# Filler matmuls between the two norms ahead of a feed-forward are left out

## The reference

```python
def rms_norm(x, g):
    y = xf * lax.rsqrt(jnp.mean(xf * xf, axis=-1, keepdims=True) + RMS_EPS)
    return (y * g.astype(jnp.float32)).astype(x.dtype)

def modulated_norm(x, g, shift, scale):
    return rms_norm(x, g) * (1 + scale) + shift

def half_step_ffn(x, g_pre, g_post, shift, scale, gate, w_gate, w_up, w_down):
    h = modulated_norm(x, g_pre, shift, scale)
    y = (jax.nn.silu(h @ w_gate) * (h @ w_up)) @ w_down
    return x + FFN_RES * gate * rms_norm(y, g_post)
```

## Time and profile before

| | us |
|---|---|
| median of 3 timed runs | 1490.08 |
| lowest, highest | 1487.72, 1493.79 |
| span of the profiled execution (no other time of it is given) | 1499.0 |
| TensorE busy in it | 1434.4 (96%) |
| VectorE busy | 979.7 (65%) |
| ScalarE busy | 621.3 (41%) |
| GpSimd busy | 121.2 (8%) |
| mean granted TensorE clock | 0.979 of full speed |

### The profile page before, as it was taken

One profiled execution on the slowest core, in us unless ns is written; L12 is line 12 of the kernel. 1 busy time (PEld: TensorE's weight loads), 2 busy tenths in 40 slices (PEclk: granted clock), 3 DMA queues, 4 the chain that ended last, 5 costly groups with the idle time before them and its releaser, 6 DMA issues.

```text
span 1499.0 us, 27870 instructions
## 1 busy us (share of the span) xinstructions
PE 1434.4 (96%) x10570; PEld 1310.5 (87%) x10570; DVE 979.7 (65%) x1425; ACT 621.3 (41%) x951; POOL 121.2 (8%) x200
## 2 busy tenths in 40 slices
PE   7899999999999999999999999999999989999997
PEld 2699999999899976589999989999876878899996
DVE  2677677777676824458787878755685785755554
ACT  2433232323465623345444455444435432544442
POOL 2000001111004002101111101100000020000000
PEclk9999999999999988999999999999999998999999
DMA  8455547777557532038888857856432432266651
GB/s 331 155 182 186 179 154 225 240 250 238 176 162 186 159 92 74 11 115 260 288 303 289 291 181 243 281 180 185 149 113 62 150 127 84 77 192 182 182 176 48
DMA packets 74482, 268.26 MB, mean 179 GB/s; under 512 B 9018, under 2 KB 9573, under 8 KB 73840
## 3 DMA queue, kind: packets, MB, share of 16 engines
q1 hardware_dynamic: 52128, 187.03, 38.4%
q0 software_dynamic: 22288, 80.30, 16.8%
HBM read 266.25 MB, written 1.05 MB: 178 GB/s over the span
## 4 chain that ended last, share of the span: by engine, by line
PE 68%; DVE 13%; issue 7%; ACT 6%; DMA 6%; DVEq 0%; ACTq 0%; SPq 0%; POOL 0%; POOLq 0%
PE gu L1372 13%; PE gu L1374 13%; PE gu L1373 13%; PE acc L1372 5%; PE acc L1374 5%; PE acc L1373 5%; DMA raw<-in_wstream_dram 5%; DVE wlo L801 4%; ACT whi L434 4%; PE mean_p L1414 2%; DVE part L818 1%; PE acc L1640 1%; DVE rstd L866 1%; PE gu L1481 1%; PE acc L1757 1%
## 5 line engine op out<-in xcount | busy, mean ns | idle before, releaser
L801 DVE TENSOR_TENSOR wlo<-raw,whi 128x1024 fp32r<-128x1024 f32 x350 | 432.9, 1242 | 284.4 <-ACT whi L434 282.9
L1372 PE MATMUL gu<-h_lat_hi,whi 128*128 128x256 f32 x1760 | 506.8, 288 | 11.6 <-DVE h_lat_lo L910 4.1
L434 ACT ACTIVATE whi<-raw 128x1024 fp32r<-128x1024 f32 x350 | 366.8, 1053 | 333.6 <-PE gu L1374 144.2
L1373 PE MATMUL gu<-h_lat_lo,whi 128*128 128x256 f32 x1760 | 500.1, 284 | 0.0
L1374 PE MATMUL gu<-h_lat_hi,wlo 128*128 128x256 f32 x1760 | 500.0, 284 | 0.0
L1372 PEld LDWEIGHTS gu<-h_lat_hi,whi 128*128 128x128 f32 x1760 | 339.8, 193 | 29.5 <-issue 17.7
L1373 PEld LDWEIGHTS gu<-h_lat_lo,whi 128*128 128x128 f32 x1760 | 340.0, 193 | 2.3 <-issue 1.7
L1374 PEld LDWEIGHTS gu<-h_lat_hi,wlo 128*128 128x128 f32 x1760 | 339.9, 193 | 0.0
L1372 PE MATMUL acc<-act_hi,whi 128*128 128x256 f32 x880 | 250.8, 285 | 3.3 <-DVE z L1140 2.6
L1373 PE MATMUL acc<-act_lo,whi 128*128 128x256 f32 x880 | 249.6, 284 | 0.0
L1374 PE MATMUL acc<-act_hi,wlo 128*128 128x256 f32 x880 | 249.5, 284 | 0.0
(11 more groups left out here) (193 smaller groups left out, 1466.2 us busy)
## 6 DMA issues: line engine op xcount, KB each, us to landing
raw<-in_wstream_dram SPq DMA_DIRECT2D x350, 512.0 KB, 4.0
wm<-in_wmod_dram POOLq DMA_DIRECT2D x136, 512.0 KB, 5.1
area<-in_wmod_dram POOLq DMA_DIRECT2D x8, 512.0 KB, 8.0
area<-in_rpb_dram POOLq DMA_DIRECT2D x32, 64.0 KB, 3.1
x_lat<-in_x_in_dram SPq DMA_DIRECT2D x1, 1024.0 KB, 8.6
area<-in_ctx_in_dram SPq DMA_DIRECT2D x1, 1024.0 KB, 12.0
area<-in_dft_in_dram POOLq DMA_DIRECT2D x1, 1024.0 KB, 8.3
area<-in_window_in_dram POOLq DMA_DIRECT2D x1, 1024.0 KB, 11.4
```

The source lines that it names most:

```text
L434: nc.scalar.activation(whi[:, phase % RING, :], raw[:, phase % RAW, :], ACT.Copy).then_inc(hi_done, 1)
L801: nc.vector.tensor_tensor(wlo[:, u.base % RING, :], raw[:, u.base % RAW, :], whi[:, u.base % RING, :].bitcast(F32), ALU.subtract).then_inc ...
L1372: nc.tensor.matmul(out_, w_hi, x_hi, start=start, stop=False, skip_group_check=True)
L1373: nc.tensor.matmul(out_, w_hi, x_lo, start=False, stop=False, skip_group_check=True)
```

## The change

The function `keep_warm`, its six calls and the constant with their number are taken out. Nothing else differs.

```diff
-            def keep_warm(n):
-
-                for _ in range(n):
-                    nc.tensor.matmul(gu[:, 1, 0:P], mean_mat[:, :], mean_mat[:, :], start=True, stop=True)
-
...
             out_projection(U_ABO, 0, (4, 5, 6, 7, 0, 1, 2, 3))
             mean_of(6)
-            keep_warm(WARM[0])
             mean_of(7)
-            keep_warm(WARM[1])
             ffn(1, 4, 4 * (6 - LATE + 1))
             mean_of(8)
             batch_columns(1)
             pe.wait_ge(act_mul, 3 * FT)
-            keep_warm(WARM[0])
             mean_of(9)
-            keep_warm(WARM[1])
...
             out_projection(U_HYO, 8, range(KT))
             mean_of(12)
-            keep_warm(WARM[0])
             mean_of(13)
-            keep_warm(WARM[1])
             ffn(3, 7, 4 * (12 - LATE + 1))
...
-WARM = [18, 18]
```

## The result

| | us |
|---|---|
| before, median of 11 runs | 1491.21 (1487.72 to 1496.37) |
| without the fillers, median of 11 runs | 1500.81 (1493.07 to 1511.07) |
| ratio, with 95% interval | 1.0052 (1.0032 to 1.0072) |

The kernel became slower by 0.52%, 7.8 us (4.8 to 10.7 us); the medians lie 9.6 us apart. The forecast was 1499.7 us, in a range of 1491 to 1504 us.

What follows compares the result with a forecast made beforehand. The prediction took TensorE, busy 96% of the span, as the bound, with the fillers off the path. Clock lags of 1.1 + 2.1 us at three places add 9.6 us to 1490.1 us: 1499.7 us, range 1491 to 1504 us.

Steps and rivals of the forecast that it cites:

- What bounds the kernel, and the direct price: Norm chain on VectorE and ScalarE paces the three places; the fillers' 25 us of TensorE lie in waits, worth zero.
- A fall in all six holes: Without fillers, TensorE idles 4.5 to 5.3 us twice at each of three places; the granted clock falls every time.
- How long the low clock lasts: From restart to rise under dense matmuls: 4.8 us, the mean of four natural cases; bounds 2.6 and 5.5 us.
- Term 1: Second norm's 16 sums at each place, run at the low clock: a lag of 1.1 us a place.
- Term 2: First matmuls of each feed-forward after a place, 0.2135 instead of 0.12 us each: a lag of 2.1 us.
- What gives it back: Later slack in the feed-forwards, weight stream included, was claimed to recover nothing of the lag.
- Sum: 1.1 + 2.1 = 3.2 us for each place, 9.6 us for three; low 3.5 us, high 11.7 us.
- The estimate of 14.4 us: Skill's rule, half the throttled time: (4.8 + 4.8) / 2 = 4.8 us a place, 14.4 us in all.
- No cost: Rival: holes don't lower the clock where it matters, or the weight stream absorbs the lag; 1490 us, chance 0.09.
- The low clock stays longer: Rival: 9.6 us of low clock at each feed-forward and sums that never warm up; 19 us, 1509 us, chance 0.09.
- Faster: Rival: a filler batch delays the real matmul behind it, likeliest at the second place; removal gives 1484 us, chance 0.03.

Runs made afterwards that it cites:

- e4_long: Kernel before with 28 fillers instead of 18 in every batch; 1497.79 us, ratio 1.0026 to the kernel before.
- e2_first_only: Kernel before with only the second filler batch of each pair left out, the first batches kept; 1501.20 us, ratio 1.0042.
- e6_late: Kernel before with 34 fillers instead of 18 in the first place's second batch, all others kept; 1495.11 us, ratio 1.0013.
- e7_place1: Kernel before with both filler batches left out at the first of the three places alone; 1497.20 us, ratio 1.0017.
- e5_half: Kernel before with 9 fillers instead of 18 in every batch; 1500.59 us, ratio 1.0055.

## Why the prediction came out right, and where it didn't

**What bounds the kernel, and the direct price.** The prediction had the fillers off the path and worth nothing themselves. Right: every other distance in the places is unchanged to 0.01 us, and e4_long shows a cost only once a batch sticks out.

**A fall in all six holes.** Right, in both profiles of the change; once, at the second place, it came 0.4 us behind the hole. The holes measured 5.17, 5.02, 4.42, 5.02, 5.17 and 5.02 us.

**How long the low clock lasts.** This step was mis-sized. I took 4.8 us from four natural rises and held it for both terms. At the start of the feed-forwards it was 4.2, 3.4 and 3.2 us in the profile of the change, and 4.1, 3.2 and 3.2 us in the second one, 3.6 us on average; from the start of the sums to the rise it was 3.2 to 5.3 us, 4.1 us on average. Three of my four rises stood behind a start that was not dense from its first record (a fall after the restart, thin matmuls, one more hole). I had counted from the restart, and at 395 us that takes in 1.4 us at the full clock: the low stretch runs from 396.4 to 399.8 us, 3.4 us and not 4.8 us.

**Term 1, the sums.** Predicted 1.1 us a place, measured 0.73 us on average over six, from 0.29 to 1.29 us. The mechanism is as told: the groups grow together and the pace of the squares hides a part, and 3.3 us of low clock over the sums at the third place leave only 0.31 us of lag.

**Term 2, the start of the feed-forward.** Predicted 2.1 us, measured 1.56 us on average, from 1.40 to 1.84 us. The rate was right: 4.2 us of low clock times (1 - 0.12 / 0.2135) gives 1.84 us, which is what the first silu shows. Only the length was off.

**What gives it back.** Predicted nothing. Right for the last feed-forward, to 0.01 us. In the feed-forward after the first place nothing was given back either; profiles with a late start are 2.3 us longer there on top of the lag. I had seen that its weight stream is nearly as slow as TensorE, and asked only whether it could absorb the lag. In `ffn(2)` the averages late and on time are alike but for the lag.

**Sum.** Predicted 3 x (1.1 + 2.1) = 9.6 us. Measured by the lags 3 x (0.73 + 1.56) = 6.9 us; the timed ratios say 7.8 us (4.8 to 10.7) and 9.1 us (4.8 to 13.5). So both terms were too large, by a third and by a half, because of the length of the low clock, and that the median came within 1.1 us of the forecast is luck. The 2.3 us seen in `ffn(1)` would bring the lags to 9.2 us; the intervals hold 6.9 and 9.2 us alike, so the timed runs don't say whether it belongs in the sum. The estimate of 14.4 us by half of the throttled time (the Trainium skill, "TensorE: Matmul & The Clock Gate", section "Terms") is above both intervals. With the lengths measured behind the two restarts, 4.1 and 3.6 us, the same rule gives an estimate of some 11.5 us, above the first interval and inside the second.

**Rivals.** "No cost" is excluded by the intervals of both runs of the change. "The low clock stays longer" didn't occur: the longest low stretch at a feed-forward's start was 5.2 us (e2_first_only, first place). "Faster" needed a batch that sticks out; at 18 fillers none does.

**What stays open.** Whether a late start costs 2.3 us in `ffn(1)`, and how, was not shown: the groups part there, `ffn(2)` does not follow, and the timed runs of e6_late and e7_place1 lie nearer to no such term. What stands out is that GpSimd's first load of modulation weights in that stretch is issued by VectorE's progress and not by TensorE's: it came 0.7 us before the first silu when the start was on time and earlier by the lag when it was late (1.7 to 3.0 us before it). The waits of TensorE that its view lists there come to 0 to 0.4 us on time and 0 to 1.1 us late, less than the 2.3 us. That the transfers collide differently is argued, not shown. How much of the array a filler has to use to hold the clock was not measured between 32 and 128 rows.

## What to carry to other kernels

A filler is worth the clock behind it, so price it where it ends: count the dense work that follows each hole and the low stretch it would run in, ask whether TensorE sets the pace there at all (at the start of this kernel it does not, and the full clock gained nothing), and check by the waits that the filler ends before its successor's operand comes. Half a batch was worth nothing here, thin fillers were worth nothing, and too long a batch cost what it stuck out; the batches that worked left 0.2 to 1.2 us of the hole. Where clock drops come at random, compare marks inside the stretch, since spans of single profiles differ by more than the effect.

## What the runs showed of the hardware that I had not expected

Much of the scatter of this kernel goes with the clock: the attention stretch had a mean granted clock of 0.88, 0.95 and 1.00 in three profiles, and norm 8's sums took 3.69 us or 5.38 us with the same code ahead of them. The wait ahead of those sums does not tell which: in the twelve profiles without fillers there it was 1.2 to 2.4 us, the three falls came behind 1.49, 1.71 and 1.89 us, and the longest kept the clock (e5_half):

```profile
874.82 3.69 PE L1414 MATMUL mean_p<-sq,mean_mat 128*128 128x256 f32 x16 [2.43 <-ACT sq L471]
```

Longer natural holes leave it open as well: the one of 2.57 us ahead of the context's down products brought the clock down in eight of the eleven profiles that leave it unfilled, and one of 3.1 us at about 525 us in eleven of thirteen. So that one profile shows no fall behind a hole does not make the hole safe. And fillers that come after the fall take long: 12 of them ran 5.49 us, where 12 of the fillers in the earlier trace rows take 2.8 us (two thirds of 4.18 us).

```profile
50.59 5.49 PE L1546 MATMUL acc<-mean_mat 128*128 128x128 f32 x24
```
